# Final norm inside the last feed-forward's block, and the second part's first weights loaded ahead

## What is computed

```python
def first_block(x, c, ...):
    for l in range(2):
        mod = silu(c) @ ada_w[l] + ada_b[l]          # six rows: sh_m, sc_m, g_m, sh_f, sc_f, g_f
        h = rms_norm(x, norm_mix_g[l]) * (1 + sc_m) + sh_m
        proj = h @ w_in[l]
        ...                                          # neighbourhood (with a bias table), latent and grouped attention
        x = x + g_m * (merged @ w_out[l])
        h = rms_norm(x, norm_ffn_g[l]) * (1 + sc_f) + sh_f
        gate, up = jnp.split(h @ ffn_w_gate_up[l], 2, axis=-1)
        x = x + g_f * ((silu(gate) * up) @ ffn_w_down[l])
    return rms_norm(x, final_norm_g)

def second_block(x, ...):
    proj = x @ w_in_2
    ...                                              # four branches, merged with gates
    x = layer_norm(DN_ALPHA * x + h, ln1_g_2, ln1_b_2)
    ...                                              # router, experts
    return layer_norm(DN_ALPHA * x + moe(x), ln2_g_2, ln2_b_2)
```

## Time and profile before

| what | us |
|---|---|
| three timed runs | 1813.05, 1820.74, 1821.10 |
| their median | 1820.74 |
| the profiled execution | 1813.24 |
| its span in the profile | 1811.3 |
| mean granted clock of PE, of full speed | 0.946 |

### The profile page before, as it was taken

The page is one execution under the profiler, slowest core; times in us unless marked ns, Lnnn a source line. Parts: engine busy times, 40 slices in busy tenths (PEclk is TensorE's granted clock), DMA queues, the critical chain, the costliest instruction groups (busy, mean ns, idle before and its releaser), DMA issues. The chain is left out here.

```text
span 1811.3 us, 25509 instructions
## 1 busy us (share of the span) xinstructions
PE 1604.7 (89%) x10701; PEld 1449.5 (80%) x10701; DVE 1227.2 (68%) x1354; ACT 816.4 (45%) x943; POOL 42.4 (2%) x60
## 2 busy tenths in 40 slices
PE   2899998999899998999969997897798958999995
PEld 2789887999798988899958997886686857888884
DVE  4877586988757557665554875534575757899895
ACT  1345533434344553443323662225433327777773
POOL 0100000000100000000000000000000000000000
PEclk9999999999999999999979998987887969999998
DMA  8975446999844324666245553111222447999992
GB/s 302 318 231 163 140 140 189 351 324 328 251 147 134 108 89 147 218 228 214 93 156 178 157 169 93 47 47 47 79 85 71 139 142 255 374 349 366 365 345 106
DMA packets 226057, 348.07 MB, mean 192 GB/s; under 512 B 14612, under 2 KB 156672, under 8 KB 225808
## 3 DMA queue, kind: packets, MB, share of 16 engines
q1 hardware_dynamic: 225936, 346.36, 57.1%
HBM read 345.29 MB, written 1.97 MB: 192 GB/s over the span
## 5 line engine op out<-in xcount | busy, mean ns | idle before, releaser
L459 PE MATMUL bank<-layer_split,hT_pair 128*128 128x256 f32 (+2 forms) x4032 | 512.7, 287 | 31.3 <-DVE hT_pair L1031 21.6
L459 PEld LDWEIGHTS bank<-layer_split,hT_pair 128*128 128x128 f32 x4032 | 486.2, 190 | 45.2 <-issue 29.9
L184 DVE TENSOR_TENSOR layer_split<-layer_raw,layer_split 128x2048 fp32r<-128x2048 f32 x122 | 279.6, 2292 | 100.8 <-ACT layer_split L172 99.4
L172 ACT ACTIVATE layer_split<-layer_raw 128x2048 fp32r<-128x2048 f32 x122 | 233.5, 1914 | 195.1 <-PE bank L459 73.7
L184 DVE TENSOR_TENSOR expert_split<-expert_raw,expert_split 128x2048 fp32r<-128x2048 f32 x96 | 219.5, 2290 | 40.7 <-ACT expert_split L172 40.6
L172 ACT ACTIVATE expert_split<-expert_raw 128x2048 fp32r<-128x2048 f32 x96 | 184.2, 1920 | 76.2 <-PE bank L2385 39.3
L459 PE MATMUL bank<-split_w,hT_pair 128*128 128x256 f32 (+1 forms) x1248 | 180.8, 308 | 13.6 <-PEq L2580 5.0
L459 PEld LDWEIGHTS bank<-split_w,hT_pair 128*128 128x128 f32 x1248 | 170.5, 204 | 24.3 <-issue 18.7
L184 DVE TENSOR_TENSOR split_w<-raw_w,split_w 128x2048 fp32r<-128x2048 f32 x52 | 119.2, 2293 | 66.2 <-ACT split_w L172 65.6
L1894 PE MATMUL bank<-layer_split,ffnh_aT 128*128 128x512 f32 x528 | 127.0, 396 | 2.8 <-DVE ffnh_aT L1962 2.8
L172 ACT ACTIVATE split_w<-raw_w 128x2048 fp32r<-128x2048 f32 x52 | 99.4, 1912 | 59.2 <-PE bank L459 50.7
(11 more groups left out here) (455 smaller groups left out, 1756.4 us busy)
## 6 DMA issues: line engine op xcount, KB each, us to landing
layer_raw<-in_ada_w SPq DMA_DIRECT2D x48, 1024.0 KB, 6.9
layer_raw<-in_ffn_w_gate_up SPq DMA_DIRECT2D x44, 1024.0 KB, 5.6
raw_w<-in_w_in SPq DMA_DIRECT2D x40, 1024.0 KB, 5.1
layer_raw<-in_w_in SPq DMA_DIRECT2D x38, 1024.0 KB, 6.1
expert_raw<-in_w_gate SPq DMA_DIRECT2D x32, 1024.0 KB, 7.1
expert_raw<-in_w_up SPq DMA_DIRECT2D x32, 1024.0 KB, 7.2
expert_raw<-in_w_down SPq DMA_DIRECT2D x32, 1024.0 KB, 6.9
layer_raw<-in_ffn_w_down SPq DMA_DIRECT2D x22, 1024.0 KB, 5.4
```

Source lines behind the costliest of these rows:

```text
L172: self.nc.scalar.activation(self.pair[:, j % self.pairs, 0, 0:self.size[n]], self.raw[:, n % self.depth, 0:self.size[n]], ACT.Copy).then_i ...
L184: self.nc.vector.tensor_tensor(self.pair[:, j % self.pairs, 1, 0:self.size[n]], self.raw[:, n % self.depth, 0:self.size[n]], self.pair[:, ...
L459: ins = nc.tensor.matmul(out, lhs, rhs, start=first and c == chunks[0] and tp + wp == 0, stop=last and c == chunks[-1] and tp == 1)
```

## The change

There are six edits of order, and some of room and of semaphores that make them possible.

1. `Projection.sync` feeds the ring through the second w_in unit before it loads the gate row and makes the strips.
2. `FeedForward.tensor`: `turn(0)` stands behind the gate products of block 1, in both layers.
3. The last layer's feed-forward gets a `RowNorm` as its next norm: squares, roots, scaling by root and gain row, transposes and splits, all ahead of the end of the block. `Norm` is gone.
4. SP loads the gain row and the second ring's first three units behind the last feed-forward unit. ACT makes the first unit's high half behind the squares and the second's behind the norm; DVE makes the first unit's low half between the two tiles. The second ring's slots lie where the merge gates and two slots of the layers' ring lay.
5. Many semaphores of the layers are one now; POOL's masks wait for two of DVE's copies of the same layer's projection as well as for the strips.
6. The second part's constants share room that ends with the mixer, so the ones that the experts' stage needs (276 columns) are loaded once more, ahead of the ln1 rows, and both PE and DVE wait for them with the router's tables.

```diff
             def sync(self, sp):
                 l, ring, w, buf = self.l, self.ring, self.w, self.buf
                 if l == 0:
-                    ring.feed(sp, ring.group_end[1] - ring.depth)
+                    ring.feed(sp, w["proj"][3] - ring.depth)
                     self.load_gate_row(sp)
                     self.make_strips(sp, 0)
...
-                pool.wait_ge(self.bias_loaded, 64)
+                pool.wait_ge(self.bias_loaded, 64 * (self.l + 1))
+                pool.wait_ge(self.dve_out.sem, 2)
...
+                    def second_ahead(sp, l=l):
+                        if l + 1 == DEPTH:
+                            sp.dma_start(gate_rows[:, 0, :], A["final_norm_g"].rearrange("(o n) -> o n", o=1)
+                                         .broadcast_to([P, D])).then_inc(gain_loaded, 16)
+                            second_ring.feed(sp, -1)
...
+        class RowNorm(SkewNorm):
...
+            def norm(self, dve, t):
+                dve.wait_ge(*self.scale_ready)
+                dve.wait_ge(self.rooted.sem, 3 * (t + 1))
+                nc.vector.scalar_tensor_tensor(x[:, t, :], x[:, t, :], rstat[:, 4 + t:5 + t], self.scale, ALU.mult, ALU.mult) \
+                    .then_inc(self.normed, 1)
...
+            def flat(self, act, t):
+                for half in range(2):
+                    hi, lo, flat, src = self.part(t, half)
+                    act.wait_ge(self.turned, 2 * t + half + 1)
+                    nc.scalar.activation(hi, src, ACT.Copy).then_inc(self.flat_out, 1)
+
+            def vector(self, dve, t):
+                for half in range(2):
+                    hi, lo, flat, src = self.part(t, half)
+                    dve.wait_ge(self.flat_out, 2 * t + half + 1)
+                    done(dve, nc.vector.tensor_copy(flat, src), self.copied)
+                    nc.vector.tensor_tensor(lo, flat, hi.bitcast(FP), ALU.subtract).then_inc(self.lo_out, 1)
...
                 self.ring.feed(sp, self.ring.ahead(self.dn(self.blocks - 1), 2))
+                self.second_ahead(sp)
...
                         hidden(n, up, t)
+                        if n == 1 and (up, t) == (0, 1):
+                            turn(0)
...
                     if n >= 1:
                         down(n - 1)
-                    turn(n)
+                        turn(n)
                 down(blocks - 1)
                 self.ada_end = ada.done_pe
+                if self.ring_next is not None:
+                    self.norm_next.turn(pe, 0)
+                    self.norm_next.turn(pe, 1)
...
+                for t, half in ((0, 0), (0, 1), (1, 0), (1, 1)):
+                    self.norm_next.square(act, t, half)
+                if self.ring_next is not None:
+                    act.wait_ge(ring.used, ring.uses(dn(self.blocks - 2)))
+                    self.ring_next.hi(act, 0)
+                for t in range(TILES):
+                    self.norm_next.flat(act, t)
+                if self.ring_next is not None:
+                    self.ring_next.hi(act, 1)
...
+                if self.ring_next is not None:
+                    norm.norm(dve, 1)
+                    norm.vector(dve, 0)
+                    self.ring_next.lo(dve, 0)
...
+                norm.vector(dve, 1)
...
                     @block.sync
                     def _(sp):
+                        sp.dma_start(tables["second"][:, :], A["constants"][:, tables["from"]:width]).then_inc(router_in, 16)
                         for i, name in enumerate(("ln1_g_2", "ln1_b_2")):
                             sp.dma_start(rows[:, i, :], A[name].broadcast_to([P, D])).then_inc(rows_in, 16)
...
-                norm = Norm("final", s2, ring, U_A[0], row_gain=gain[:, :], late_gain=(gain_loaded, 16), junk=work_[:, 0, :])
-                project("mix_in", ring, jobs, banks=7, norm=norm,
+                project("mix_in", ring, jobs, banks=7,
```

236 lines of the change are left out of this document (96 added, 140 removed).

## The result

| | us |
|---|---|
| kernel before, median of 13 runs | 1816.04 (1813.05 to 1821.85) |
| kernel after, median of 13 runs | 1823.06 (1818.14 to 1826.71) |
| ratio after to before | 1.0032, 95% interval 1.0016 to 1.0048 |
| profiled execution after | 1823.04, span 1821.3, clock 0.945 |

The change makes the kernel slower by 7.0 us in the medians; by the ratio's interval it is 2.9 to 8.7 us, so the direction is clear over 13 runs. The forecast was 7.7 us faster. The time is 10.1 us above the forecast 1813.0 and above the range's end of 1820, and the starting point hides part of the miss: the 1820.74 that I took over was a high median of three, and thirteen runs give 1816.04. In the difference the miss is 14.7 us. The two profiles are 10 us apart; that of before stands at the low end of its runs.

The account below looks back on a forecast made before the run. PE, busy 89% of the span, was taken as the bound, so time is won only where it waits. Six terms summed to -7.7 us, giving 1813.0 against the median of 1820.74; range 1801 to 1820.

Parts of the forecast that it names:

- 1 start: Kernel start: w_in units ahead of the strips bring the first product to 43.97 us and the late landing forward; -4.5 us.
- 2 turn(0), second layer: Second layer's feed-forward: PE's 2.67 us wait before the first transposes is filled with block 1 products; -2.7 us.
- 3 turn(0), first layer: First layer's feed-forward: second transposes stay at 317.9 us, the wait gathers, slow products fall behind it; +1.6 us.
- 4 passage: Passage from layers to second part: norm and transposes done in the old block, first product at 930.6 us; -2.2 us.
- 5 masks: Second layer: POOL's masks no longer run beside DVE's split of the norm before PE's first product; -0.4 us.
- 6 tables: Router: the extra 128x276 load ahead of ln1's rows makes DVE wait longer, 3.3 us for the rows; +0.5 us.
- My lower bound of 2.2: Start: smallest gain allowed, 2.2 us, if the unit behind the strips lands only at 53.4 us.
- Rival (c): Start: strips behind w_in units block SP, third unit lands at 62 us; +4.8 in all, 1825.5 us; chance 0.06.
- Rival (d): First layer: the gap is filled because the next gate unit lands earlier, -3.7 for +1.6, 1807.7 us; chance 0.05.
- The chance that unit 3 comes too late: Passage: second ring's unit 3 comes 2.5 late and eats the gain; part of a 1817.8 us rival, chance 0.15.
- The chain that I laid out: Passage: last root at 919.46, norms to 920.75, DVE copies, subtractions and low half to 928.5, first product 930.6 us.

Follow-up runs that it names:

- b3: Kernel before with only the first edit: ring fed through the second w_in unit ahead of gate row and strips; 1820.45 us, 1.0020 of before.
- a5: `a4_down_place` with the first edit undone too, so the strips come ahead of the first w_in unit; 1807.27 us, 0.9938 of before.
- b4: Kernel before with only the second edit, turn(0) behind two halves of block 1 in both layers; 1817.14 us, 1.0008 of before.
- a3: Kernel after with the first layer's turn(0) undone, tables reloaded later, and 160 bytes of padding ahead of the merge gates; 1806.94 us, 0.9949 of before.
- a6: Kernel after with every edit kept, five small tiles (160 bytes) moved ahead of the merge gates; 1810.07 us, 0.9961 of before.
- a1: Kernel after with 32 bytes per partition put ahead of the merge gates, nothing else; 1815.22 us, 0.9985 of before.
- a4_down_place: a3 with its 160 bytes of padding replaced by five small tiles, returning the turned activations to their old place; 1806.22 us, 0.9929 of before.
- b5: Kernel before with one pad of 128 bytes ahead of the layers' split slots; 1824.85 us in one execution.

## Why the prediction was wrong, point by point

| term | forecast | bounds | measured | from |
|---|---|---|---|---|
| 1 start | -4.5 | -6.2 to -2.2 | 0 | after, b3, a5 |
| 2 turn(0), second layer | -2.7 | -2.7 to 0 | -2.7 | b4, a3 to a6 |
| 3 turn(0), first layer | +1.6 | -3.7 to +2.1 | +1.9 | 4 profiles with, 12 without |
| 4 passage | -2.2 | -4.3 to 0 | -2.9 | 7 profiles with, 9 without |
| 5 masks | -0.4 | -0.4 to 0 | 0 | 16 profiles |
| 6 tables | +0.5 | 0.3 to 0.8 | +0.7 | after, a1, a6, 13 without |
| not in the sum: place of the split slots | | | +10.3 | after against a6 |
| sum | -7.7 | | +7.3 | |

The edits alone add up to -3.0. The measured total is +7.0; that the sum comes so near is in part luck, since the stretch behind the passage, where two executions of the kernel before differ by 5.7 us, isn't in it.

**The missing term.** Edit 4 of the change puts the second ring's slots where the merge gates and two slots of the layers' ring lay, and I read that as a matter of when memory is free. The prediction counts six edits of the order and puts the edits of room at nothing, without a reason. That is the step that failed: they moved the weights that PE streams in every block. From the first Sigmoid of the first feed-forward to the last `down` it takes 614.4 us in `a6_only_place` and 624.7 in the kernel after, which differ in nothing but placement: 10.3 us, of which 3.4 lie in the first feed-forward, 4.1 in the second and 2.8 between them (where profiles of equal placement differ by up to 2). The rows of the feed-forwards in the trace of before couldn't show it, since all their blocks have one pace. But the same trace has a second pace for products of the same shape out of other slots: 192 in 23.02 us, so 96 in 11.51 against 11.14. The sum took every duration of before over to a program with other addresses, and said nothing of that. The range of 1801 to 1820 had no room for it. Without it the same terms give 3.0 us faster, still less than half of the 7.7, because of part 1.

**1, the start.** This is the second step that failed: -4.5 forecast, 0 measured. The shift of the chain to the first product was right to 0.2 us. What failed is "From 51, less some 1.5 us in which DMA had just run empty before": I counted the hole at 30 to 40 us as bandwidth won, though the strips' traffic, which made the hole, was only put elsewhere. My lower bound of 2.2 was no bound for the same reason. Rival (c), that the strips block SP behind w_in units, had the third unit at 62 us; it was 55.72, below its point of decision of 57. The strips took SP 8.02 us, less than the 10.96 of before.

**2, second layer.** Right: 2.7 forecast, 2.7 measured in `b4_turn` and in `a3` to `a6`, which have the edit and the old pace.

**3, first layer.** Right in mechanism and nearly in size. The second transposes stayed (317.71), the gap gathered, and the products behind it ran slow. The Trainium skill says in "TensorE: Matmul & The Clock Gate", in the part on oscillation of the clock gate in real kernels, that waits for DMA between short groups of products take the clock down, so that the next group starts slow. The trace agrees: a granted clock of 0.50 from 316 to 322 us, and 13.21 us for 96 products that take 11.45 in later blocks. The edit would have been right in the second layer alone. Rival (d) is out.

**4, the passage.** Right: 24.3 to 24.6 us from the last `down` in the other kernels without the edit, and 24.24 in the first trace, against 21.5 in all seven with it. The products come 15.7 us after the last one has ended (938.43 - 922.77), 16.3 forecast. The chance that unit 3 comes too late didn't come true. The chain that I laid out ends 22.0 us after the start of the last `down` (930.6 against 908.59), the real one 21.5.

**5, masks.** From the last `down` to the products of the second tile 24.1 to 25.3 us without the edit, 23.6 to 24.9 with it. The mechanism was there: PE waits 3.14 us before the first product in the five profiles without the edit in which POOL's masks ran beside that instruction, and 2.74 in the other four and in all seven with the edit. But the masks fell there in only half of the executions, and by the second tile no gain can be told.

**6, tables.** 7.7, 8.0 and 8.5 us from the last add to the rows' use, without the load 7.1 to 7.6: 0.7 in the mean, inside the bounds. The 2.7 us that the router lost on top in the profile after are not of this term: the 32 products ran at the lower clock all through in four of the 16 profiles, three of them without the load (`b3`, `b4`, `b5`).

## What to carry to other kernels

When an edit moves or frees memory, list the address of every large operand that PE streams, before and after, and treat a changed remainder as an edit of its own: its price here (10 us) was more than all the edits of order together, forecast or measured. Test it with a kernel that moves tiles by a few bytes and no instruction. And a stretch of low DMA rate that is caused by small pieces is not free bandwidth: ask where those pieces go, and look at the landing that ends last, not at the first product.

## What the runs showed of the hardware

- The pace of PE's products at full granted clock depends on where their operands lie in a partition: 11.14 to 11.75 us for 96 products of 256 columns, 5.63 to 5.77 for 24 of 512, with the remainders of the table above. In some places it changes from block to block of one program and holds all through a block. The second part shows the same: 192 products out of its split slots take 23.02 us with the slots at 0 modulo 256 and 22.02 at 64. The Trainium skill gives in "TensorE: Matmul & The Clock Gate", in the part on the back-to-back issue gap, a formula for the spacing that has only the number of columns in it; the rows here differ by 5% at the same number of columns. The Trainium skill says in "SBUF — State Buffer", in the part on the two separate sides, that PE's port never waits on anyone; no run here shows where the time is lost, so this is neither confirmed nor refuted.
- An earlier arrival can be worth less than it looks: `a4_down_place` came into the second part 2.2 us earlier than `a3_place` and had 0.2 left at 1012 us, since PE's clock came back at about the same time in both (0.65 and 0.64 in the stretch 930 to 935 us, 1.00 from 935), and was lower again in `a4_down_place` at 975 to 980 us.
